# Moving five blocks of h and the forget sums to other turns of a hand-written order (decoder layer, f32, one core)

## The chip, the cores and the metric

The kernel runs on one core of a Trainium2 chip. The time is that of the device in microseconds (us) for one launch, median of several runs. In the profile, PE is TensorE's matmuls and PEld its weight loads, DVE is VectorE, ACT ScalarE, POOL GpSimd, and SP the engine that issues most DMAs; a q behind a name is the engine's queue of issues.

## The reference

One layer of a decoder over 256 tokens of width 2048: a projection into the inputs of three kinds of mixers, their outputs projected back, and an MLP.

```python
mod = (silu(c) @ w_mod[l] + b_mod[l])[:, None, :]
sh1, sc1, g1, sh2, sc2, g2 = jnp.split(mod, 6, axis=-1)
h = rms_norm(x, norm1_g[l]) * (1.0 + sc1) + sh1
(fq, fk, fv, ff, nq, kc, vc, ksl, vsl, kwn, vwn, ng, ca, cg) = split_in(h @ w_in[l])
log_f = jax.nn.log_sigmoid(ff + b_f[l])
o_fox = fox_attention(hd(fq), hd(fk), hd(fv), log_f)   # adds F[t] - F[s], F = cumsum(log_f)
o_nsa = nsa_attention(...)
o_conv = conformer_conv(ca, cg, ...)
x = x + g1 * (concat([o_fox, o_nsa, o_conv]) @ w_out[l])
h = rms_norm(x, norm2_g[l]) * (1.0 + sc2) + sh2
x = x + g2 * (jnp.square(jax.nn.relu(h @ w_mlp1[l])) @ w_mlp2[l])
```

## The kernel before

All products with weights are made in three parts, high by high, high by low and low by high, in a 32-bit format of TensorE (fp32r). So each piece of weights that arrives in `raw` is split: ScalarE copies it into `w_hi` (`weight_hi`, line 749), and VectorE takes the difference into `w_lo` (`weight_lo`, line 1497). The unit of this is a half: 1024 columns of 128 rows, two rows of tiles deep. There are four buffers each of `w_hi` and `w_lo`, so ScalarE may write `w_hi` of half n when TensorE has done half n-4. TensorE takes 24 matmuls of 256 columns for a half that gives results by feature (lines 1059 to 1061), 12 matmuls of 512 columns for one by token (lines 1083 to 1085), and short ones of 176 columns for the group TL.

The input projection has 88 halves. They go in units over quarters of the depth: halves 0 to 21 use blocks 0 and 1 of h (a block is two tiles of 128 features), halves 22 to 37 blocks 2 and 3, halves 38 to 45 blocks 4 and 5, halves 46 to 53 blocks 6 and 7, and from half 54 on units use several. TL has halves 20, 21, 28 and 29 in the stretch of interest.

The order of all engines is written out by hand. TensorE goes through slots, with half n in slot n. ScalarE, VectorE and SP go through turns; in turn n they treat half n of the weights, some three halves ahead of TensorE. Each engine does its instructions in order, and what it needs of another it waits for by semaphore. In a turn:

- ScalarE first copies the result of a unit that has ended, then makes a block of h if `H_AT` names one for this turn (`scale_shift`, lines 754 to 765), then writes `w_hi`, then makes the four products of a tap of the convolution (`conv_products`, line 789, turns 56 and on).
- VectorE adds the result of a unit that has ended, writes `w_lo`, adds a tap (line 1604), splits the block that ScalarE made a turn before (`split_h`, line 1552), and last takes products with modulation weights.

A block of h needs the modulation's shift and scale as columns. VectorE makes them: `modulation_column` (line 1504) multiplies 128 rows of `w_mod` with the row of silu(c) and sums (2.2 us), four of them make a block, and behind the fourth VectorE's `scale_shift` writes `scale_h` (line 1529) and counts up `col_ok`. By `MODS_AT` there is one such product in each odd turn and two in turns 9, 21, 27 and 33. The fourth product of blocks 2 to 7 falls into turns 9, 17, 23, 29, 35 and 43. ScalarE's part begins so:

```python
def scale_shift(b):
    act.wait_ge(col_ok, b + 1)
    act.wait_ge(xt_ok, b + 1)
    if b >= 2:
        act.wait_ge(h_ready, b - 1)
```

The forget gates' running sums are eight small matmuls (`forget_sums`, lines 1264 to 1274) in slot `F_SLOT`. In turn `F_SLOT + AHEAD` (AHEAD is 3) VectorE splits them into `f_split` (lines 1785 to 1797). The first scores of the FoX heads, in slot 72, wait for that (`f_sb`, line 1219), as `f_split` is an operand of theirs. VectorE then adds the mask and takes the maximum (line 1632, first in turn 75), ScalarE takes the exponential (line 812), and TensorE transposes (line 1244) in slot 73.

All weights are issued by SP on one queue in the order of the turns: in each odd turn two halves of weights (1 MB), behind a wait for a `w_lo` that frees `raw`, and for each product of modulation weights the next load into its buffer (1 MB, line 550), behind a wait for that product.

Of the kernel before, what the change touches and what calls it, by code (L numbers as in the profile page):

```python
# [126 lines left out]
TAIL_TURN = TAIL_SLOT + AHEAD  # L127

LF_TURN = FIRST_HALF[UNITS.index((FE, 3, 1, 2, False, True)) + 1] + 4
F_SLOT = 64  # L130
MIX_SLOTS = [FOX_AT + 6, FOX_AT + 10, FOX_AT + 14, NSA_SLOT + 14, NSA_SLOT + 17, TAIL_SLOT + 1]
GATE_SLOTS = [NSA_SLOT + t for t in (18, 19, 20, 21)]
MIX_TURNS = [n + AHEAD for n in MIX_SLOTS]
# [62 lines left out]
    return 32 + 2 * i  # L196


H_AT = {12: 2, 20: 3, 27: 4, 33: 5, 39: 6, 45: 7}


def view(ap, dims, shift=0):
# [4 lines left out]
def build(nc, x_d, c_d, wmod_d, bcol_d, bmod_d, n1_d, n2_d, fg_d, main_d, tail_d, bf_d, wck_d, wcv_d, pos_d,  # L207
# [6 lines left out]
    with ctx:  # L214
# [484 lines left out]
        def _(act):  # L699
# [54 lines left out]
# [6 lines that stand above are left out]
                for k in (2 * b, 2 * b + 1):  # L760
                    A(h_f[b % 2][:, (k % 2) * S:(k % 2 + 1) * S], xn_t[:, k, :], ACT.Identity,
                      bias=m_sum[:, 2 * k:2 * k + 1], scale=scale_h[:, k:k + 1]).then_inc(h_ok, 1)
                act.wait_ge(h_ok, 2 * b + 2)
                A(act_hi[:, 2 * b:2 * b + 2, :], h_f[b % 2][:, :].rearrange("p (k t) -> p k t", k=2), ACT.Copy)\
                    .then_inc(h_hi, 1)
# [87 lines left out]
            for turn, (half, step) in enumerate(TURNS):  # L853
# [9 lines left out]
                if turn == TAP_HALF - 1:  # L863
                    act.wait_ge(small_in, 16 * N_SMALL)
                    act.wait_ge(evac_add, added(CG))
                    A(conv_y[:, :, :], conv_y[:, :, :], ACT.Sigmoid).then_inc(conv_sig, 1)
                if turn in H_AT:
                    scale_shift(H_AT[turn])
                if half is not None:
# [179 lines left out]
        def _(pe):  # L1049
# [214 lines left out]
            def forget_sums():  # L1264

                pe.wait_ge(lf_ok, 1)
                pe.wait_ge(evac_add, added(FE))
                for base in (0, HD):
                    out = spare[base:base + NFOX, 0:3 * P]
                    mm(out[:, 0:P], log_f[:, 0, :], tri[:, :], start=True, stop=True)  # L1270
                    mm(out[:, P:2 * P], log_f[:, 0, :], tri[:, :], start=True, stop=True)
                    mm(out[:, 2 * P:3 * P], log_f[:, 0, :], ones[:, :], start=True, stop=False)
                    last = mm(out[:, 2 * P:3 * P], log_f[:, 1, :], tri[:, :], start=False, stop=True)
                last.then_inc(f_ps, 1)
# [43 lines left out]
            for slot, (half, step) in enumerate(SLOTS):  # L1318
# [17 lines left out]
                if slot == 3:  # L1336
                    pe.wait_ge(bias_row, 1)
                if slot == F_SLOT:
                    forget_sums()
# [142 lines left out]
        def _(dve):  # L1482
# [66 lines left out]
            def split_h(b):  # L1549
                dve.wait_ge(h_hi, b + 1)  # L1550
                src = h_f[b % 2][:, :].rearrange("p (k t) -> p k t", k=2)
                TTn(act_lo[:, 2 * b:2 * b + 2, :], src, act_hi[:, 2 * b:2 * b + 2, :].bitcast(f32),
                    ALU.subtract).then_inc(h_ready, 1)
# [34 lines left out]
            def add_tap(tap):  # L1588

                if tap < 0:  # L1590
                    dve.wait_ge(conv_sig, 1)
                    TTn(conv_in[:, :, CONV_W - 1:], conv_in[:, :, CONV_W - 1:], conv_y[:, :, :], ALU.mult)\
                        .then_inc(conv_sem, 1)
                elif tap in VECTOR_TAPS:
                    dve.wait_ge(conv_sem, tap)
                    for ct in range(CT):
                        last = STT(conv_y[:, ct, :], conv_in[:, ct, tap:tap + S], convw[:, ct, tap:tap + 1],
                                   conv_y[:, ct, :], ALU.mult, ALU.add)
                    last.then_inc(conv_sem, 1)
                elif tap > 0:  # L1600
                    n = SCALAR_TAPS.index(tap)
                    dve.wait_ge(conv_tap, n + 1)
                    dve.wait_ge(conv_sem, tap)
                    TTn(conv_y[:, :, :], conv_y[:, :, :], conv_p[n % 2][:, :, :], ALU.add).then_inc(conv_sem, 1)  # L1604
# [133 lines left out]
            for turn, (half, step) in enumerate(TURNS):  # L1738
# [21 lines left out]
                if 0 < turn - TAP_HALF - 1 < CONV_W:  # L1760
                    add_tap(turn - TAP_HALF - 1)
                if turn - 1 in H_AT:
                    split_h(H_AT[turn - 1])
                if turn == LF_TURN:
# [5 lines left out]
                if turn == LF_TURN + 2:  # L1770
# [13 lines left out]
                    STT(log_f[:, :, :], s, -2.0, lf[0][:, :, :], ALU.mult, ALU.add).then_inc(lf_ok, 1)  # L1784
                if turn == F_SLOT + AHEAD:

# [365 lines left out]
```

## Time and profile before

| | |
|---|---|
| median of 3 runs | 1215.96 us (1215.74 to 1217.17) |
| profiled execution, its own time | 1217.17 us |
| its span, first to last instruction | 1215.4 us |
| mean granted TensorE clock | 0.975 of 2.4 GHz |
| TensorE busy | 1163.8 us, 96% |
| VectorE busy | 896.3 us, 74% |
| ScalarE busy | 605.8 us, 50% |

The span is from the first instruction to the last; the execution's time holds 1.8 us around it. A granted clock of 0.50 means 1.2 GHz. Busy shares are means over stages of different kinds; the input projection is the first 280 us or so.

### The profile page before, as it was taken

How to read it: one execution, taken by the hardware profiler on the slowest of the kernel's cores; microseconds unless marked ns; L12 is line 12 of the kernel's file. 1: busy time of each engine (PE TensorE's matmuls, PEld its weight loads, DVE VectorE, ACT ScalarE, POOL GpSimd, SP SyncE). 2: the span in 40 equal slices, each digit the busy share in tenths (PEclk: the TensorE clock that was granted, in tenths of full speed). 3: DMA queues.
4: the chain of work that ended last, by engine and by line, in shares of the span. 5: the costliest groups of instructions: out<-in, count | busy, mean ns of one | idle time of the engine just before them, and what ended most of it. 6: DMA issues, size and time to landing. Idle time of an engine off the chain costs nothing.

```text
span 1215.4 us, 17307 instructions
## 1 busy us (share of the span) xinstructions
PE 1163.8 (96%) x6807; PEld 1009.9 (83%) x6807; DVE 896.3 (74%) x1011; ACT 605.8 (50%) x874; POOL 10.5 (1%) x29
## 2 busy tenths in 40 slices
PE   4999999999999996999999999999999999999997
PEld 4899989988877775999788888888888888888785
DVE  5998999998889978896865666545666545667674
ACT  6655448876754544544433444433444433444452
POOL 2000000000000000000000000000000000000000
PEclk6999999999989997999999999999999999999998
DMA  9999996538856875986667664555665456665441
GB/s 380 419 420 420 420 365 251 179 142 295 277 208 250 298 317 210 355 308 242 231 229 261 242 236 179 186 195 210 259 225 204 173 196 238 238 227 178 169 173 69
DMA packets 45752, 306.11 MB, mean 252 GB/s; under 512 B 6316, under 2 KB 7928, under 8 KB 9208
## 3 DMA queue, kind: packets, MB, share of 16 engines
q1 hardware_dynamic: 43728, 302.58, 66.0%
q10 hardware_dynamic: 1896, 2.64, 0.8%
q8 instruction: 43, 0.70, 0.2%
q14 instruction: 21, 0.17, 0.0%
q0 software_dynamic: 64, 0.02, 0.0%
HBM read 303.10 MB, written 2.12 MB: 251 GB/s over the span
## 4 chain that ended last, share of the span: by engine, by line
PE 77%; DVE 10%; ACT 5%; issue 5%; DMA 3%; SPq 0%; DVEq 0%; ACTq 0%
PE quad L1069 15%; PE quad L1083 12%; PE quad L1085 12%; PE quad L1084 12%; PE quad L1071 7%; PE quad L1059 5%; PE quad L1060 5%; PE quad L1061 5%; DMA mod_raw<-in_w_mod 3%; DVE w_lo L1497 2%; ACT w_hi L749 2%; DVE mod_raw L1504 2%; DVE conv_y L1604 1%; ACT score L812 1%; ACT conv_p L789 1%
## 5 line engine op out<-in xcount | busy, mean ns | idle before, releaser
L1497 DVE TENSOR_TENSOR w_lo<-raw,w_hi 128x1024 fp32r<-128x1024 f32 (+1 forms) x372 | 446.8, 1208 | 263.8 <-ACT w_hi L749 263.2
L749 ACT ACTIVATE w_hi<-raw 128x1024 fp32r<-128x1024 f32 (+1 forms) x372 | 387.4, 1045 | 424.0 <-PE quad L1085 218.9
L1069 PE MATMUL quad<-act,w_hi 128*128 128x512 f32 x768 | 268.1, 394 | 0.0
L1059 PE MATMUL quad<-act,w_hi 128*128 128x256 f32 x768 | 223.1, 291 | 8.7 <-DVE w_lo L1497 4.6
L1060 PE MATMUL quad<-act,w_hi 128*128 128x256 f32 x768 | 220.8, 287 | 0.0
L1061 PE MATMUL quad<-act,w_lo 128*128 128x256 f32 x768 | 220.7, 287 | 0.0
L1071 PE MATMUL quad<-act,w_lo 128*128 128x256 f32 x768 | 215.4, 280 | 0.0
L1083 PE MATMUL quad<-w_hi,u_hi 128*128 128x512 f32 x496 | 196.4, 396 | 0.5 <-DVE u_lo L1914 0.5
L1085 PE MATMUL quad<-w_hi,u_lo 128*128 128x512 f32 x496 | 195.9, 395 | 0.0
L1084 PE MATMUL quad<-w_lo,u_hi 128*128 128x512 f32 x496 | 195.9, 395 | 0.0
L1069 PEld LDWEIGHTS quad<-act,w_hi 128*128 128x128 f32 x768 | 144.2, 188 | 33.4
L1059 PEld LDWEIGHTS quad<-act,w_hi 128*128 128x128 f32 x768 | 150.1, 195 | 11.5 <-issue 8.8
L1060 PEld LDWEIGHTS quad<-act,w_hi 128*128 128x128 f32 x768 | 150.2, 196 | 0.2
L1061 PEld LDWEIGHTS quad<-act,w_lo 128*128 128x128 f32 x768 | 150.0, 195 | 0.0
L1071 PEld LDWEIGHTS quad<-act,w_lo 128*128 128x128 f32 x768 | 144.5, 188 | 0.1
L1083 PEld LDWEIGHTS quad<-w_hi,u_hi 128*128 128x128 f32 x496 | 93.0, 187 | 23.8 <-DVE u_lo L1914 0.9
L1084 PEld LDWEIGHTS quad<-w_lo,u_hi 128*128 128x128 f32 x496 | 93.0, 187 | 22.7 <-issue 0.2
L1085 PEld LDWEIGHTS quad<-w_hi,u_lo 128*128 128x128 f32 x496 | 93.0, 187 | 22.7
L1504 DVE CUSTOM_DVE_ANT_0 mod_raw<-mod_raw,acc 128x2048 f32<-128x2048 f32 x40 | 91.3, 2287 | 12.7 <-ACT acc L725 7.6
L1515 DVE SCALAR_TENSOR_TENSOR acc<-mod_raw,c_act,acc 128x2048 f32<-128x2048 f32 x32 | 75.1, 2346 | 0.0
L812 ACT ACTIVATE score<-score,neg_max 128x128 f32<-128x128 f32 x72 | 31.9, 444 | 52.5 <-DVE neg_max L1632 52.5
L789 ACT ACTIVATE conv_p<-conv_in,convw 128x256 f32<-128x256 f32 x108 | 45.8, 496 | 8.9 <-DVE conv_y L1604 8.9
(288 smaller groups left out, 1161.0 us busy)
## 6 DMA issues: line engine op xcount, KB each, us to landing
raw<-in_w_main SPq DMA_DIRECT2D x184, 1024.0 KB, 4.8
mod_raw<-in_w_mod SPq DMA_DIRECT2D x72, 1024.0 KB, 6.6
first_raw<-in_w_mod SPq DMA_DIRECT2D x14, 1024.0 KB, 14.1
late_raw<-in_w_mod SPq DMA_DIRECT2D x10, 1024.0 KB, 7.6
x_a<-in_x SPq DMA_DIRECT2D x2, 1024.0 KB, 6.9
x<-in_x SPq DMA_DIRECT2D x2, 1024.0 KB, 8.6
out<-raw SPq DMA_DIRECT2D x4, 512.0 KB, 3.1
bias_t<-bias_scratch ACTq DMA_DIRECT2D x1, 1536.0 KB, 15.2
```

Source lines behind the costliest of these rows:

```text
L749: A(dst[:, 0:2 * width], block_half(raw, j, width), ACT.Copy).then_inc(hi_done, 1)
L1059: mm(out, hi, act_hi[:, k, :], start=begin and m % 2 == 0, stop=False, skip_group_check=True)
L1060: mm(out, hi, act_lo[:, k, :], start=False, stop=False, skip_group_check=True)
L1061: last = mm(out, lo, act_hi[:, k, :], start=False, stop=end, skip_group_check=True)
L1069: mm(out, w_hi[j % 4][:, cols], act_both[:, k, :, :].rearrange("p h t -> p (h t)"), start=begin, stop=False, skip_group_check=True)
L1071: last = mm(out[:, 0:S], w_lo[j % 4][:, cols], act_hi[:, k, :], start=False, stop=end, skip_group_check=True)
L1083: mm(out, t_hi, hi, start=begin, stop=False)
L1084: mm(out, t_hi, lo, start=False, stop=False)
L1085: last = mm(out, t_lo, hi, start=False, stop=end)
L1497: TTn(lo[:, 0:2 * width], block_half(raw, j, width), hi[:, 0:2 * width].bitcast(f32), ALU.subtract)\
L1504: v.tensor_tensor_reduce(out=src[:, :], in0=src[:, :], in1=acc[0][:, :], scale=1.0, scalar=0.0, op0=ALU.mult, op1=ALU.add, accum_out=m_col ...
L1515: STT(out, src[:, :], c_act[:, bass.ds(k, 1)], out, ALU.mult, ALU.add).then_inc(mod_step, 1)
```

## The change

Two constants of the written order are changed. The keys of `H_AT` are the turns in which ScalarE makes a block, the values the blocks; VectorE's `split_h` comes one turn after.

```diff
-F_SLOT = 64
+F_SLOT = 70
 MIX_SLOTS = [FOX_AT + 6, FOX_AT + 10, FOX_AT + 14, NSA_SLOT + 14, NSA_SLOT + 17, TAIL_SLOT + 1]
 GATE_SLOTS = [NSA_SLOT + t for t in (18, 19, 20, 21)]
...
-H_AT = {12: 2, 20: 3, 27: 4, 33: 5, 39: 6, 45: 7}
+H_AT = {12: 2, 18: 3, 24: 4, 30: 5, 36: 6, 44: 7}
```

Which block is made in which turn, and when its columns are made and the block is needed:

| block | columns, VectorE's turn | made, before | made, after | first needed by half |
|---|---|---|---|---|
| 2 | 9 | 12 | 12 | 22 |
| 3 | 17 | 20 | 18 | 23 |
| 4 | 23 | 27 | 24 | 38 |
| 5 | 29 | 33 | 30 | 39 |
| 6 | 35 | 39 | 36 | 46 |
| 7 | 43 | 45 | 44 | 47 |

## Rows read from the trace of the kernel before

**Rows 1.** The page: the span, and TensorE's busy time.

```profile
span 1215.4 us, 17307 instructions
...
PE 1163.8 (96%) x6807; PEld 1009.9 (83%) x6807; DVE 896.3 (74%) x1011; ACT 605.8 (50%) x874; POOL 10.5 (1%) x29
```

**Rows 2.** Waits, 50 to 155 us: us in total, times, longest.

```profile
DVE mod_raw L1504 <- DMA mod_raw<-in_w_mod: 2.8, 4, 1.5
...
PE quad L1059 <- DVE w_lo L1497: 2.3, 1, 2.3
```

**Rows 3.** Timeline of ScalarE: start, us, operation, count, [idle before, releaser].

```profile
90.14 1.06 ACT L749 ACTIVATE w_hi<-raw 128x1024 fp32r<-128x1024 f32 x1 [0.25 <-PE quad L1085]
...
99.71 1.43 ACT L749 ACTIVATE w_hi<-raw 128x1024 fp32r<-128x1024 f32 x2
...
105.72 1.06 ACT L749 ACTIVATE w_hi<-raw 128x1024 fp32r<-128x1024 f32 x1 [1.49 <-PE quad L1061]
...
112.16 1.09 ACT L761 ACTIVATE h_f<-xn_t,m_sum,scale_h 128x256 f32<-128x256 f32 x2 [0.39 <-DVE scale_h L1529]
...
113.82 1.04 ACT L749 ACTIVATE w_hi<-raw 128x1024 fp32r<-128x1024 f32 x1
...
123.78 1.06 ACT L749 ACTIVATE w_hi<-raw 128x1024 fp32r<-128x1024 f32 x1 [1.78 <-PE quad L1061]
...
132.22 1.06 ACT L749 ACTIVATE w_hi<-raw 128x1024 fp32r<-128x1024 f32 x1
```

**Rows 4.** Timeline of VectorE, 83 to 131 us.

```profile
83.69 0.53 DVE L1497 TENSOR_TENSOR w_lo<-raw,w_hi 128x352 fp32r<-128x352 f32 x1 [1.19 <-ACT w_hi L749]
...
94.03 2.35 DVE L1497 TENSOR_TENSOR w_lo<-raw,w_hi 128x1024 fp32r<-128x1024 f32 x2
...
100.79 1.23 DVE L1497 TENSOR_TENSOR w_lo<-raw,w_hi 128x1024 fp32r<-128x1024 f32 x1 [1.05 <-ACT w_hi L749]
...
106.80 0.68 DVE L1552 TENSOR_TENSOR act<-h_f,act 128x512 fp32r<-128x512 f32 x1
...
109.43 2.29 DVE L1504 CUSTOM_DVE_ANT_0 mod_raw<-mod_raw,acc 128x2048 f32<-128x2048 f32 x1 [1.51 <-DMA mod_raw<-in_w_mod]
...
112.04 2.35 DVE L1497 TENSOR_TENSOR w_lo<-raw,w_hi 128x1024 fp32r<-128x1024 f32 x2
...
121.83 2.29 DVE L1504 CUSTOM_DVE_ANT_0 mod_raw<-mod_raw,acc 128x2048 f32<-128x2048 f32 x1 [0.65 <-DMA mod_raw<-in_w_mod]
...
129.53 2.36 DVE L1497 TENSOR_TENSOR w_lo<-raw,w_hi 128x1024 fp32r<-128x1024 f32 x2
```

**Rows 5.** Timeline of TensorE, and a window with its granted clock (PEclk).

```profile
113.41 0.36 PE L1059 MATMUL quad<-act,w_hi 128*128 128x256 f32 x1 [2.30 <-DVE w_lo L1497]
...
115.27 0.41 PE L1059 MATMUL quad<-act,w_hi 128*128 128x256 f32 x1
...
115.00:116.00 1.00, 1.00 (x7) 1.00 (x6) 1.00 (x1) 0.00 (x0) 0.00 (x0) 0.50 1.08 451
```

**Rows 6.** SP's issue, and a window (last two: DMA share, GB/s).

```profile
98.63 0.33 SPq L550 DMA_DIRECT2D mod_raw<-in_w_mod  x1
...
100.00:104.00 4.00, 4.00 (x36) 4.00 (x35) 3.21 (x2) 2.32 (x4) 0.00 (x0) 1.00 1.02 420
```

**Rows 7.** Timelines of TensorE and VectorE around the first scores.

```profile
216.62 0.38 PE L1059 MATMUL quad<-act,w_hi 128*128 128x256 f32 x1
...
222.03 0.17 DVE L1790 CAST neg_id_r<-neg_id 128x12 fp32r<-128x12 f32 x1
...
225.00 1.23 DVE L1497 TENSOR_TENSOR w_lo<-raw,w_hi 128x1024 fp32r<-128x1024 f32 x1
...
239.53 0.44 PE L1231 MATMUL quad<-f_split,neg_id_r 44*128 44x384 f32 x2
...
243.54 0.28 DVE L1632 CUSTOM_DVE_ANT_0 score<-quad,causal 128x128 f32<-128x128 f32 x1
...
245.25 0.55 PE L1244 MATMUL quad<-ident,score 128*128 128x128 f32 x3 [1.59 <-ACT score L812]
```

## The prediction

> **What bounds the kernel now.** I read the page first. TensorE is busy for 1163.8 of 1215.4 us, so what the change does to the end is what it does to TensorE's waits and clock [rows 1]. The change touches two stretches of the input projection, so I listed the waits of 50 to 155 us. TensorE waits there for a single thing: 2.3 us, for a `w_lo` of VectorE; and VectorE waits 2.8 us in all for modulation weights to land [rows 2]. I then put the timelines of ScalarE and VectorE side by side and gave each `w_hi` and `w_lo` its number by counting turns. TensorE runs half n in slot n; ScalarE writes `w_hi` of half n once half n-4 is done (so a `w_hi` that waited for TensorE tells when that half ended), and VectorE then writes `w_lo` of half n. VectorE is the full engine: two `w_lo` (1.14 us each from start to start), a product of modulation weights (2.2 us) and now and then a `split_h` (0.60) stand against two halves of TensorE (5.6 to 5.7 us), and in four turns of the stretch there are two products. So TensorE sets the pace with VectorE about a microsecond ahead of it, and any idle time of VectorE over that goes to TensorE.
>
> The one stall shows the pattern. VectorE waits 1.51 us for weights to land, starts the product at 109.43, and starts `w_lo` of half 30 at 112.04 [rows 4]; TensorE, idle since about 110.94, starts half 30 at 113.41, 1.37 us after that `w_lo` began, and then runs at a granted clock of 0.50, 1.2 of 2.4 GHz, for 3.4 us [rows 5]. Seventeen matmuls came 0.213 apart where 0.118 is usual, so the lower clock costs another 1.6 us behind the 2.3.
>
> **H_AT, removed and added.** No operation is added or taken away. Blocks 3 to 7 of h are made at turns 18, 24, 30, 36, 44 where they were at 20, 27, 33, 39, 45, and their `split_h` moves with them. TensorE needs them much later (halves 23, 38, 39, 46, 47), so being earlier is worth nothing by itself. What matters is what `scale_shift` on ScalarE waits for: the columns `scale_h` of its block, which VectorE writes at the end of turns 17, 23, 29, 35 and 43. Four of the five moves put the block into the very next turn (18, 24, 30, 36), and so does 44. In before, ScalarE runs ahead: it wrote `w_hi` of half 24 at 90.14, of half 30 at 105.72 and of half 36 at 123.78 [rows 3], while VectorE started the `w_lo` behind the columns of these blocks at 94.03, 112.04 and 129.53 [rows 4]. In the changed kernel these `w_hi` stand on ScalarE behind a wait for those columns. Queued behind the waiting instruction are `w_hi` of that half and the next ones, and VectorE's next instruction is the `w_lo` of just that half: the two engines, which ran side by side, run one after the other.
>
> The price of one such place comes from block 5 in turn 33. From the start of the product (109.43) to `h_f` on ScalarE (112.16) are 2.73 us, from there to the next `w_hi` (113.82) 1.66 [rows 3, 4], and a `w_lo` starts 1.08 behind its `w_hi` (99.71 and 100.79): 5.47 us. Today it is 2.61 (109.43 to 112.04). So VectorE idles 2.86 us more at each of turns 18, 24, 30, 36, and at 44 too, where the cover is greater.
>
> Against that, VectorE loses idle time it has now: 1.19 us at half 21 (it waits for ScalarE, which waits for TensorE), 1.05 at half 27 (ScalarE was at block 4 in that turn), 1.51 and 0.65 for weights to land [rows 4]: 4.4 us, which are swallowed by its being late. 0.73 us comes on at half 31, as in that turn a copy of a result stands between `w_hi` 30 and 31 on ScalarE. I carried it through turn by turn, as shift against before of the start of each operation:
> - `w_lo` 18: +2.86. `w_lo` 20: +3.48 (its `split_h` is now ahead of it). `w_lo` 22: +1.61 (1.19 swallowed, `split_h` gone from behind 21, small gaps). It starts at 90.77; TensorE gets it at 92.14 and is ready at 91.24: a stall of 0.9.
> - `w_lo` 24: +4.49, start 98.52, TensorE gets it at 99.89 and is ready at 97.82: a stall of 2.1.
> - `w_lo` 27: +3.96. Product before block 5: at 111.21, the landing wait of 1.51 gone: +1.78. `w_lo` 30: +4.64, start 116.68. TensorE gets it at 118.05 where it got it at 113.41: it is 4.6 us behind before, whatever its clock did in between, as this chain is on VectorE and ScalarE alone.
> - `w_lo` 32: +5.89; `w_lo` 34: +5.17 (landing wait of 0.65 and small gaps swallowed); `w_lo` 35: +4.57; `w_lo` 36: +7.43, start 136.96.
> TensorE gets half 36 at 138.33. Today it starts it at 131.98 (ScalarE saw half 35 end at 132.22 [rows 3], less 0.24, the lag seen at half 30), 1.08 after it could. So TensorE is 7.43 - 1.08 = 6.35 us late there. It would be ready at 136.6, with the lower clock after half 30 in it: a stall of about 1.7. The stall of 1.59 us at 245.25 is followed by the lower clock as well [rows 7], so I add 1.6: +8.0 us from half 37 on. At turn 44 the columns come late once more; `w_lo` 44 reaches TensorE at 160.2, and it needs it at 160.9 at the earliest: no stall. From turn 47 VectorE again waits for ScalarE and TensorE, so all three are 8.0 us late, and nothing later is tied to a fixed time that could give it back. Of the clock I can bound only this: 0 if the last stall is too short, 1.6 if not, 3.3 if it takes two such stretches.
>
> One thing is tied to fixed times: weights land by their place in the queue. The product's weights were issued at 98.63 and landed at 109.43, 10.8 us later [rows 6], while the DMA share is above 1.00 throughout (this issue alone moves 1 MB, 2.5 us at 420 GB/s): the rest is backlog. In the changed kernel that issue comes about 5 us later, at 103.7, behind a queue that is still full until 106.9, so I leave the landing at 109.43, before the 111.21 at which it is wanted. The Trainium skill (DMA: Bandwidth & Descriptors, section "Two DMAs through the same engine are not ordered") says that within one queue of one engine descriptors start in order though they are pipelined. By this the landing is set by the bytes ahead, and the sum stays as it is; were the 10.8 us a latency of its own, the landing would be 114.5 and the sum 3.3 us more.
>
> The skill has a rule that speaks for a smaller sum: TensorE: Matmul & The Clock Gate, section "Why this matters for your kernels", ties drops of throughput in mid-kernel to idle gaps longer than any in my list. By it none of my stalls costs clock, and the sum would be 6.35. The row at 113.41 shows otherwise after 2.30 us, and the measurement decides.
>
> **F_SLOT.** The eight forget sums (1.42 us of TensorE, up to the start of half 64 at 216.62) and VectorE's six passes for `f_split` (2.97 us, 222.03 to 225.00) move six turns on, to slot 70 and turn 73 [rows 7]. What has to wait for them is the first score in slot 72, which started at 239.53. Told on before's times: without the passes `w_lo` 68 to 73 move up, but VectorE then soon waits for ScalarE, whose turn of tap products takes 2.55 us where VectorE's takes 2.27, so that `w_lo` 73 starts at 235.9 instead of 238.71, the tap behind it ends at 238.17 and `f_split` at 241.14. The scores start at 241.37 where TensorE is free at 239.35: a new wait of 2.0 us. The bias of these scores starts on VectorE at 243.42, before at 243.54. TensorE has a wait of 1.59 us in front of the transposes at 245.25 and a lower clock behind it; both are now spent one slot earlier: half 72 ends at 245.24 + 1.7 = 246.9, and the transposes stand where they stood in effect (245.25 + 1.7). I take 0. Bounds: -1.15, all of VectorE's idle time from 222.03 to 243.54, and +2.0, if the new wait is added whole.
>
> **Sum.** 6.35 + 1.6 + 0 = +8.0 us. The profiled execution took 1217.17 us around its span of 1215.4, 1.2 above the median of 1215.96; so I expect 1225.2 for that one and 1224.0 for the median.
>
> **Rivals.**
> - *The serial turns, but the clock holds* after the last stall: 6.35, 1222.3. For it: that stall is the shortest of the three large ones. Against it: 245.25.
> - *Dearer*: landings move with their issue (+3.3), the slot 72 wait is added whole (+2.0), or a second slow stretch (+1.7): 1226 to 1229.
> - *Half of it hidden*: VectorE's margin ahead of TensorE takes up more than the 1.08 us that I counted, or one of the turns isn't serial: 1219 to 1221.
> - *No change, the blocks' wait hidden*: that wants the columns before the `w_hi`; the row at 112.16 with its 0.39 us of waiting, three turns later than it would be asked, is against it. 1216.
> - *Faster*: with block 4 out of turn 27 VectorE saves its wait of 1.05 at half 27, and with its `split_h` (0.60 at 106.80) out of turn 28 it is 1.65 us earlier at `w_lo` 30; the stall of 2.30 falls to 0.65 and the 1.6 of clock go with it: 1215.96 - 3.25 = 1212.7. This decides only if the columns of block 5 are there before about 105.7, where `w_hi` 30 stands, 6.4 us earlier than the trace has them.
>
> **How the numbers follow.** Forecast 0.55, clock holds 0.14, dearer 0.11, half hidden 0.09, no change 0.05, faster 0.06. A change under 0.2% (2.4 us) can't be told from none here. Slower is 0.89, same 0.05, faster 0.06. The range from 1219.5 to 1228.5 leaves out the last two, the lower edge of the half-hidden case and the upper one of the dear case.
>
> **What would show it.** Right: ScalarE's `h_f` waits for `scale_h` at blocks 3 to 7, each time followed by a `w_lo` that waits about 2.9 us for `w_hi`; waits of TensorE for `w_lo` at halves 24, 30 and 36 of 2.1, 2.6 and 1.7 us and a granted clock of 0.50 behind each; half 36 at 138.3; from turn 50 everything later by one constant; a wait of 2.0 us before the first score. The prediction is wrong if landings of weights end VectorE's waits, if half 36 starts before 136, or if the 8 us are there at 160 and gone at 460.

## The result

| | before | after |
|---|---|---|
| median, us | 1215.85 (6 runs, 1214.73 to 1217.17) | 1221.16 (6 runs, 1220.16 to 1223.61) |
| ratio, 95% interval | | 1.0051, 1.0040 to 1.0062 |
| profiled execution, its own time | 1217.17 | 1221.82 |
| its span | 1215.4 | 1220.1 |
| mean granted clock | 0.975 | 0.979 |

The changed kernel is 0.5% slower, 5.3 us by the medians, where 8.0 were forecast. The ratio is taken over all 15 of its timed runs, whose mean is 1222.0 us; by it the difference is 6.2 us, with an interval of 4.9 to 7.5. For the same reason a ratio and a difference of medians below can differ by some tenths of a us. The page of after, against [rows 1]:

```profile
span 1220.1 us, 17307 instructions
...
PE 1159.6 (95%) x6807; PEld 1005.9 (82%) x6807; DVE 895.7 (73%) x1011; ACT 604.0 (50%) x874; POOL 10.5 (1%) x29
```

TensorE's busy time is even 4.2 us lower, since it spent less time at the low clock and had a faster pace late in the kernel (see *Spans* below). The longer span is idle time. The waits from 50 to 155 us (us in total, times, longest), against [rows 2]:

```profile
ACT h_f L761 <- DVE scale_h L1529: 27.4, 5, 7.5
...
DVE w_lo L1497 <- ACT w_hi L749: 11.7, 5, 2.8
PE quad L1059 <- DVE w_lo L1497: 7.0, 3, 3.9
...
PE quad L1083 <- DVE w_lo L1497: 1.5, 1, 1.5
...
DVE mod_raw L1504 <- DMA mod_raw<-in_w_mod: 0.6, 2, 0.4
```

TensorE waits 8.5 us for `w_lo` where it waited 2.3. VectorE's waits for weights have shrunk from 2.8 to 0.6 us, swallowed by its lateness. ScalarE now stands before a block of h for up to 7.5 us. Its timeline, at blocks 4 and 5, against [rows 3]:

```profile
95.59 1.09 ACT L761 ACTIVATE h_f<-xn_t,m_sum,scale_h 128x256 f32<-128x256 f32 x2 [6.48 <-DVE scale_h L1529]
...
97.25 2.94 ACT L749 ACTIVATE w_hi<-raw 128x1024 fp32r<-128x1024 f32 x3
...
113.70 1.09 ACT L761 ACTIVATE h_f<-xn_t,m_sum,scale_h 128x256 f32<-128x256 f32 x2 [6.64 <-DVE scale_h L1529]
```

And VectorE's, against [rows 4]: the `w_lo` of halves 18, 24, 30 and 36, each behind the same wait.

```profile
80.21 2.36 DVE L1497 TENSOR_TENSOR w_lo<-raw,w_hi 128x1024 fp32r<-128x1024 f32 x2 [2.78 <-ACT w_hi L749]
...
98.33 2.36 DVE L1497 TENSOR_TENSOR w_lo<-raw,w_hi 128x1024 fp32r<-128x1024 f32 x2 [2.77 <-ACT w_hi L749]
...
110.98 2.28 DVE L1504 CUSTOM_DVE_ANT_0 mod_raw<-mod_raw,acc 128x2048 f32<-128x2048 f32 x1
...
116.43 1.23 DVE L1497 TENSOR_TENSOR w_lo<-raw,w_hi 128x1024 fp32r<-128x1024 f32 x1 [2.77 <-ACT w_hi L749]
...
136.67 2.36 DVE L1497 TENSOR_TENSOR w_lo<-raw,w_hi 128x1024 fp32r<-128x1024 f32 x2 [2.77 <-ACT w_hi L749]
...
249.67 0.29 DVE L1632 CUSTOM_DVE_ANT_0 score<-quad,causal 128x128 f32<-128x128 f32 x1
```

The row at 113.70 is the pattern in one line: ScalarE had been ready for 6.64 us, VectorE wrote the columns, waited 2.77 us for the `w_hi` behind them, and only then had work again. TensorE, against [rows 5, 7], with three windows of it (the third number from the end is the granted clock):

```profile
91.96 0.36 PE L1059 MATMUL quad<-act,w_hi 128*128 128x256 f32 x1 [1.36 <-DVE w_lo L1497]
...
99.70 0.36 PE L1059 MATMUL quad<-act,w_hi 128*128 128x256 f32 x1 [1.81 <-DVE w_lo L1497]
...
117.80 0.36 PE L1059 MATMUL quad<-act,w_hi 128*128 128x256 f32 x1 [3.87 <-DVE w_lo L1497]
...
138.04 0.48 PE L1083 MATMUL quad<-w_hi,act 128*128 128x512 f32 x1 [1.54 <-DVE w_lo L1497]
...
211.13 0.36 PE L1059 MATMUL quad<-act,w_hi 128*128 128x256 f32 x1 [2.27 <-DVE w_lo L1497]
...
247.30 0.44 PE L1231 MATMUL quad<-f_split,neg_id_r 44*128 44x384 f32 x2 [3.08 <-DVE f_split L1795]
```

```profile
100.00:101.00 1.00, 1.00 (x11) 1.00 (x10) 1.00 (x2) 1.00 (x2) 0.00 (x0) 1.00 0.96 401
...
120.00:122.00 2.00, 2.00 (x12) 2.00 (x11) 2.00 (x2) 0.50 (x1) 0.00 (x0) 0.50 0.89 340
...
139.00:140.00 1.00, 1.00 (x6) 0.77 (x6) 1.00 (x3) 0.48 (x1) 0.00 (x0) 1.00 0.32 131
```

There are four waits at halves 22, 24, 30 and 36, as worked out, but the clock fell behind one of them alone, that of 3.87 us (it fell once more behind the 3.08 us before the first scores). Half 36 starts at 138.04. In the projection TensorE is then 6.1 us late; the wait at half 61 stands at 211.13 where it stood at 205.00, and the first mask and maximum at 249.67 where it was at 243.54, both 6.13 us later.

### The profile page after: what moved, and what is told of

It is laid out like the page before. It is cut to its first block, busy times and chain, and to the rows that moved or that the text cites. A ratio compares the mean times of both kernels' runs of the same rounds, so it can differ in the third digit from the quotient of the medians.

```text
span 1220.1 us, 17307 instructions
## 1 busy us (share of the span) xinstructions
PE 1159.6 (95%) x6807; PEld 1005.9 (82%) x6807; DVE 895.7 (73%) x1011; ACT 604.0 (50%) x874; POOL 10.5 (1%) x29
## 4 chain that ended last, share of the span: by engine, by line
PE 70%; DVE 15%; ACT 7%; issue 5%; DMA 3%; SPq 0%; DVEq 0%; ACTq 0%
PE quad L1069 14%; PE quad L1083 11%; PE quad L1084 11%; PE quad L1085 11%; PE quad L1071 7%; DVE w_lo L1497 4%; PE quad L1059 3%; PE quad L1060 3%; PE quad L1061 3%; DVE mod_raw L1504 3%; ACT w_hi L749 2%; DMA mod_raw<-in_w_mod 2%; DVE first_raw L1504 2%; DVE conv_y L1604 1%; ACT conv_p L789 1%
```

## The experiments

Each was timed against the kernel before on the same chip. The medians of before were 1215.88 us beside the two parts apart, the repeat and block 6 alone; 1215.78 beside block 3 alone, all blocks one turn later and the first move of modulation products; and 1215.59 beside the other four. Theory A is that of the prediction: ScalarE and VectorE run one after the other in the turns in which a block waits for its columns, and VectorE's loss less what its later idle time swallows goes to TensorE. Its main rival B puts the cost to the new wait before the first scores.

### The two parts apart

```diff
-H_AT = {12: 2, 20: 3, 27: 4, 33: 5, 39: 6, 45: 7}
+H_AT = {12: 2, 18: 3, 24: 4, 30: 5, 36: 6, 44: 7}
```

> The five blocks are moved and the forget sums stay in slot 64. Theory A (the serial turns of VectorE and ScalarE carry all of the change): VectorE's wait for w_hi at halves 18, 24, 30 and 36 is 2.8 us each, TensorE starts half 36 at about 138.0 as in the changed kernel, and the time is 4.5 to 6.5 us over before. Rival B (the cost is the new wait of 3.08 us in front of the first scores): the time is within 2.4 us of before. Clock: the waits of TensorE at halves 22, 24 and 36 (1.4, 1.8, 1.5 us) will be followed by the lower clock in some executions and not in others, so this run need not match the changed kernel's profile there.

Measured 1222.27 us, ratio 1.0057 (1.0045 to 1.0070), 6.4 us over before. TensorE starts half 36 at 138.12.

```diff
-F_SLOT = 64
+F_SLOT = 70
```

> The forget sums are moved to slot 70 and the blocks stay where they were. Theory A: a new wait of TensorE of 2.0 to 3.1 us for f_split before the first scores, the wait of 1.59 us before the first transposes gone, the first mask and maximum on VectorE (before at 243.54) within 0.3 us of that, and the time within 1.2 us of before. Rival B: the new wait is added whole, 2 to 3 us over before.

Measured 1216.20 us, ratio 1.0001 (0.9992 to 1.0010). Its timeline of TensorE has the new wait before the first scores:

```profile
242.63 0.69 PE L1231 MATMUL quad<-f_split,neg_id_r 44*128 44x384 f32 x2 [3.09 <-DVE f_split L1795]
```

A wait of 3.09 us that costs nothing: the mask and maximum stands at 245.00, 38.56 us behind the end of the wait at half 61 (206.44). In before these are 38.54 (243.54 less 205.00), in after 38.54 (249.67 less 211.13). I had expected that row within 0.3 us of the 243.54 of before, and missed it: the whole execution was 1.44 us later from half 61 on. The wait of 1.59 us at the transposes is gone, as expected. Rival B falls: the blocks alone give all of the change's cost, and the forget sums none that shows within an interval of -1.0 to 1.2 us.

### The changed kernel once more

> The changed kernel itself again, for another sample of the clock. Theory C (which of the short waits is followed by the lower clock is chance, not set by the length of the wait): waits of the same length at halves 22, 24, 30 and 36 within 0.2 us where no fall comes before them, and another set of falls behind them than in the first profile (there: behind 3.87 us yes, behind 1.36, 1.81 and 1.54 no). Rival D (a wait is followed by a fall from some length on): the same set. Time 1220 to 1224.

Measured 1222.83 us, ratio 1.0060 (1.0048 to 1.0072). TensorE's waits in the new profile, and a window behind the first:

```profile
92.21 0.36 PE L1059 MATMUL quad<-act,w_hi 128*128 128x256 f32 x1 [1.34 <-DVE w_lo L1497]
...
99.95 0.36 PE L1059 MATMUL quad<-act,w_hi 128*128 128x256 f32 x1 [0.29 <-DVE w_lo L1497]
...
118.07 0.55 PE L1059 MATMUL quad<-act,w_hi 128*128 128x256 f32 x1 [3.86 <-DVE w_lo L1497]
...
138.31 0.47 PE L1083 MATMUL quad<-w_hi,act 128*128 128x512 f32 x1 [0.72 <-DVE w_lo L1497]
...
247.59 0.44 PE L1231 MATMUL quad<-f_split,neg_id_r 44*128 44x384 f32 x2 [1.54 <-DVE f_split L1795]
...
93.00:94.00 1.00, 1.00 (x6) 1.00 (x6) 1.00 (x2) 0.00 (x0) 0.00 (x0) 0.50 1.01 421
```

The same 1.3 us of waiting at half 22 is followed by the clock of 0.50 here and was not in the first profile. TensorE lost time to it, and found `w_lo` 24 nearly ready: 0.29 us of waiting and not 1.81. Halves 30 and 36 start 25.86 and 46.10 us after half 22, against 25.84 and 46.08 in the first profile. So ScalarE and VectorE set these starts, and a low clock between two waits costs nothing there; only one behind the last wait would. That holds even for the wait at half 30, in which the clock fell before it ended and stayed low for 6.8 us, twice as long as in the first profile. Behind half 36 the clock held in all three profiles of these blocks (after, its repeat, the blocks alone; the waits there were 1.54, 0.72 and 1.53 us). Rival D falls for the short waits. All of TensorE's waits over 1 us between 85 and 255 us, in the profiles of before, after, its repeat and the two parts apart, and then in all thirteen profiles of this case (a fall is counted that came in the wait or up to 1.6 us behind it):

| wait, us | clock fell, these five | clock fell, all thirteen |
|---|---|---|
| 1.25 to 1.69 (halves 22, 30, 32, 34 and 36, scores) | in 2 of 7 | in 5 of 15 |
| 1.81 to 1.97 (halves 24 and 30) | in 1 of 2 | in 3 of 4 |
| 2.26 to 2.34 (halves 30, 36 and 61) | in 4 of 7 | in 10 of 17 |
| 2.53 to 2.55 (scores) | in 1 of 1 | in 2 of 4 |
| 2.91 to 3.87 (half 30, scores) | in 5 of 5 | in 7 of 7 |

### One block alone

```diff
-H_AT = {12: 2, 20: 3, 27: 4, 33: 5, 39: 6, 45: 7}
+H_AT = {12: 2, 20: 3, 27: 4, 33: 5, 36: 6, 45: 7}
```

> Only block 6 is moved, from turn 39 to 36. Theory A: one serial turn, 2.8 us of new waiting of VectorE for w_hi at half 36, of which TensorE's distance of 1.08 us takes a part: TensorE waits 1.7 to 1.8 us at half 36 for w_lo, and the time is 1.3 to 2.0 us over before, 3.4 with the lower clock behind the wait. Rival (the cost needs all moves together, one is absorbed): 0.

Measured 1218.16 us, ratio 1.0014 (1.0005 to 1.0023), over before by 2.3 us by the medians and 1.7 by the ratio. VectorE's wait is there:

```profile
132.56 2.36 DVE L1497 TENSOR_TENSOR w_lo<-raw,w_hi 128x1024 fp32r<-128x1024 f32 x2 [2.77 <-ACT w_hi L749]
```

TensorE waits 0.89 us and not 1.7 for it in this profile, since its own wait at half 30 was 3.05 us, the clock fell in it and stayed low for 6.8 us, and that had made TensorE later. The interval of 0.6 to 2.8 us holds the 1.8 of the sum and leaves out the rival's 0.

```diff
-H_AT = {12: 2, 20: 3, 27: 4, 33: 5, 39: 6, 45: 7}
+H_AT = {12: 2, 18: 3, 27: 4, 33: 5, 39: 6, 45: 7}
```

> Only block 3 is moved, from turn 20 to 18. Theory A (a serial turn costs only what VectorE's later idle time does not swallow): TensorE gets a new wait of about 0.9 us at half 22, VectorE's waits of 1.05 us at half 27 and of 1.51 us for the weights that land at 109.43 shrink by as much, the wait of TensorE at half 30 shrinks from 2.30 to about 1.4 us, half 30 starts at 113.4 as before, and the time is that of before within 1 us. Rival (each serial turn costs its own 1.8 us): 1.5 to 2 us over before.

Measured 1214.62 us, ratio 0.9989 (0.9980 to 0.9997): no cost, 1.2 us less if anything. The timeline of VectorE:

```profile
80.67 2.36 DVE L1497 TENSOR_TENSOR w_lo<-raw,w_hi 128x1024 fp32r<-128x1024 f32 x2 [2.78 <-ACT w_hi L749]
...
102.03 1.23 DVE L1497 TENSOR_TENSOR w_lo<-raw,w_hi 128x1024 fp32r<-128x1024 f32 x1 [0.40 <-ACT w_hi L749]
...
109.63 2.29 DVE L1504 CUSTOM_DVE_ANT_0 mod_raw<-mod_raw,acc 128x2048 f32<-128x2048 f32 x1 [0.47 <-DMA mod_raw<-in_w_mod]
```

And that of TensorE:

```profile
92.42 0.36 PE L1059 MATMUL quad<-act,w_hi 128*128 128x256 f32 x1 [0.72 <-DVE w_lo L1497]
...
113.60 0.36 PE L1059 MATMUL quad<-act,w_hi 128*128 128x256 f32 x1 [1.25 <-DVE w_lo L1497]
```

The same 2.78 us of VectorE's time is lost, and paid back from the waits at half 21 (gone, 1.19 in before), at half 27 (0.40 for 1.05) and for weights (0.47 for 1.51). The product starts at the landing, 109.63 (in before 109.43), and half 30 starts at 113.60. TensorE's one wait of 2.30 is split into 0.72 and 1.25 and no low clock follows in this profile. From the start of half 30 to the end of the wait at half 61 are 90.74 us here (204.34 less 113.60) and 91.59 in before, so the missing fall is worth 0.85 us. The profile is ahead by more than that at its end, 3.3 us; half of it, 1.7 us, comes from a faster pace of TensorE behind 664 us that doesn't go with the blocks (see *Spans* below). Whether the 1.2 us of the medians are real isn't shown.

### The place of the wait

```diff
-H_AT = {12: 2, 20: 3, 27: 4, 33: 5, 39: 6, 45: 7}
+H_AT = {12: 2, 19: 3, 25: 4, 31: 5, 37: 6, 45: 7}
```

> Blocks 3, 4, 5, 6, 7 in turns 19, 25, 31, 37, 45, one turn after the changed kernel's, with the forget sums in slot 64. Theory A: when ScalarE waits for the columns, the w_hi of the turn in which they are made is already there, so VectorE does one w_lo (1.14 us) in the meantime and waits 1.7 us and not 2.8 in each of four places. 4 x 1.7 less the 4.4 that are swallowed, less the distance of 1.08: 1 to 3 us over before, so well under the time of the kernel with all moves. Rival (what costs is that the blocks are early at all): 4.5 to 6.5 us over before.

Measured 1216.41 us, ratio 1.0004 (0.9995 to 1.0013), 0.6 us over before where 1 to 3 were expected. VectorE waits 1.63 to 1.65 us for `w_hi` in the four places; at block 4:

```profile
97.54 1.23 DVE L1497 TENSOR_TENSOR w_lo<-raw,w_hi 128x1024 fp32r<-128x1024 f32 x1 [1.65 <-ACT w_hi L749]
```

One turn makes 5.8 us of difference to the blocks alone in the changed kernel's turns.

Now with the changed kernel's turns and ScalarE's order within a turn reversed:

```diff
-H_AT = {12: 2, 20: 3, 27: 4, 33: 5, 39: 6, 45: 7}
+H_AT = {12: 2, 18: 3, 24: 4, 30: 5, 36: 6, 44: 7}
...
-                if turn in H_AT:
-                    scale_shift(H_AT[turn])
                 if half is not None:
                     weight_hi_in(half)
+                if turn in H_AT:
+                    scale_shift(H_AT[turn])
```

> The blocks in the changed kernel's turns 18, 24, 30, 36, 44, the forget sums in slot 64, and one edit: in each turn ScalarE writes w_hi first and makes the block behind it. Theory A (the cost is that w_hi of just the half that VectorE wants next stands behind the wait for the columns): each serial turn leaves VectorE waiting 1.6 us and not 2.8, as with all blocks one turn later, and the time is within 2 us of before, 4 to 6 us under the kernel with the same turns and the old order. Rival (it is the turns in which the blocks stand): 1221 to 1223 as with the old order.

Measured 1217.70 us, ratio 1.0021 (1.0012 to 1.0031), 2.1 us over before: just outside of the 2 us expected, and 4.3 us less over its before than the blocks alone in the old order. VectorE's waits are 1.64, 1.65, 2.55 and 1.64 us, the second of them:

```profile
97.25 1.23 DVE L1497 TENSOR_TENSOR w_lo<-raw,w_hi 128x1024 fp32r<-128x1024 f32 x1 [1.65 <-ACT w_hi L749]
```

It is not the turns, but what stands behind the wait. The 2.55 at half 31, where a copy of a result comes in between, I hadn't counted.

```diff
-H_AT = {12: 2, 20: 3, 27: 4, 33: 5, 39: 6, 45: 7}
+H_AT = {12: 2, 20: 3, 26: 4, 32: 5, 38: 6, 45: 7}
```

> Blocks 4, 5 and 6 one turn before where the kernel before has them (26, 32, 38), nothing else. Theory A: the columns of all three are written or nearly so when ScalarE comes there, so no wait of VectorE for w_hi over 1.7 us appears; the wait of 1.05 us at half 27 goes; the weights still land at 109.4 to 109.8 and set half 30; the time is that of before within 1.2 us.

Measured 1216.22 us, ratio 1.0006 (0.9998 to 1.0015): no difference, as expected. VectorE's wait at half 27 is gone and comes back in front of the weights (2.83 us for 1.51). They land at 109.52, and half 30 starts where it did:

```profile
113.50 0.55 PE L1059 MATMUL quad<-act,w_hi 128*128 128x256 f32 x1 [2.91 <-DVE w_lo L1497]
```

This answers the prediction's rival *Faster* as well: with block 4 out of turn 27 half 30 is no earlier, as the product before it has to wait for the landing.

### Whether another order is faster

```diff
+MODS_AT = {turn + (turn == 29): n for turn, n in MODS_AT.items()}
```

> Before with one edit: the product with modulation weights of turn 29 (the one that VectorE waits for until 109.43) is done at the end of turn 30, behind w_lo of half 30. Theory A (VectorE does its work in order, and w_lo 30 stands behind a load that lands late): w_lo 30 starts at about 107.9 and not at 112.04, the wait of TensorE at half 30 (2.30 us) goes, w_lo 31 is just in time, and with the lower clock behind it 2.3 to 4 us are saved: 1212 to 1213.7. Rival (the wait only moves on to half 31 or 32, since VectorE's work is the bound there): within 1 us of before.

Measured 1214.74 us, ratio 0.9988 (0.9979 to 0.9997), where 1212 to 1213.7 were expected. The wait at half 30 is gone, and two others have come, at halves 32 and 34 (the next expectation miscounts the second as 35):

```profile
118.27 0.36 PE L1060 MATMUL quad<-act,w_hi 128*128 128x256 f32 x1 [1.50 <-DVE w_lo L1498]
...
125.73 0.47 PE L1084 MATMUL quad<-w_hi,act 128*128 128x512 f32 x1 [1.54 <-DVE w_lo L1498]
```

They are 3.04 us in all for 2.30, so the 1.0 us that the median gains isn't less waiting. In this profile the clock fell behind neither of them nor at half 61; in before it fell at halves 30 and 61. That may be where the gain comes from, but one profile doesn't show it.

```diff
+MODS_AT = {turn: n for turn, n in MODS_AT.items() if turn not in (29, 31, 33)} | {30: 1, 32: 1, 33: 1, 34: 1}
```

> Before with the products of turns 29, 31 and 33 (one, one, two) in turns 30, 32, 33 and 34 (one each), so that w_lo of the half that TensorE wants is not behind a load that lands late. With the product of turn 29 alone moved, the wait of 2.30 us at half 30 went and waits of 1.50 and 1.54 us at halves 32 and 35 came. Theory A (the order of work decides): those shrink to 1 us or less in sum, 1212.5 to 1214. Rival (VectorE with the landing times is the bound of this stretch, the order only moves the waits): 1214 to 1215.5.

Measured 1214.94 us, ratio 0.9997 (0.9988 to 1.0006). The waits have moved on once more, to halves 35 (125.69, 0.47 us) and 36 (131.04, 2.31 us). With blocks 3 and 4 at turns 19 and 26 as well:

```diff
-H_AT = {12: 2, 20: 3, 27: 4, 33: 5, 39: 6, 45: 7}
+H_AT = {12: 2, 19: 3, 26: 4, 33: 5, 39: 6, 45: 7}
```

> As the run before, and blocks 3 and 4 at turns 19 and 26. If the order decides, no slower than the run before, and ScalarE's block is out of turn 27; if landings decide, the same within 0.8 us. A price of the serial turn at 19 (1.6 us of VectorE) should be swallowed by waits for weights behind it.

Measured 1216.64 us, ratio 1.0003 (0.9993 to 1.0014). This is 1.7 us over the run before and so fits neither expectation, though the intervals of the two ratios overlap. In its profile the clock fell behind all three waits of TensorE over 1 us (131.11, 205.76 and 246.01), in that of the run before behind one, which may be the difference. The rival holds as far as the first two of these kernels show it: moving the products moves the waits about (2.30; 1.50 and 1.54; 0.47 and 2.31) and takes none away, so the stretch is bound by VectorE's work with the landing times. No version beat the kernel before by more than the 0.2% that can be told here; the two lowest ratios are 0.9988 and 0.9989, with intervals up to 0.9997.

## Why the prediction was right, and its one wrong term

- *The serial turns.* Right in kind, place and size. VectorE idles 2.77 to 2.78 us at halves 18, 24, 30 and 36 where 2.86 more were worked out; `w_lo` 24, 30 and 36 start at 98.33, 116.43 and 136.67 against 98.52, 116.68 and 136.96; half 36 starts at 138.04 against 138.33. At half 44 VectorE waits 2.78 us as well (159.24), and no wait of TensorE follows, as forecast. Undoing the order in the turn and moving the blocks by one turn took away 4 to 6 us, and the blocks alone gave all of it.
- *What swallows it.* Right: the waits at halves 21 and 27 and for the weights are gone in after; block 3 alone costs nothing, block 6 alone, behind which no such idle time stands, does.
- *The landing.* Right: with block 3 alone the load was issued at 100.52, 1.89 us later than in before, and the product started at its landing, 109.63 for 109.43. In after the load was issued at 103.53 and the product of block 5's columns is at 110.98 (111.21 worked out) with no wait, 7.5 us later; a latency of 10.8 us from the issue, which would have added 3.3 us, falls by that.
- *The waits of TensorE.* At half 22 1.36 for 0.9, at half 24 1.81 for 2.1, at half 30 3.87 for 2.6, at half 36 1.54 for 1.7. The one at 22 came out longer since TensorE was 0.6 us earlier in this execution (ready at 90.60 for the 91.22 of before), the one at 30 since the low clock that I had put behind half 24 did not come. A clock of 0.50 behind each of 24, 30 and 36 was named as a sign of being right; it came behind 30 alone.
- *The clock behind half 36*, "so I add 1.6: +8.0 us". This is the term that was mis-sized: it measured 0 in all three profiles. The single row I had, a wait of 1.59 us before the transposes with a low clock behind it, was one throw. At its own place it was a fair guide, as the clock fell at waits of 1.58 to 1.69 us there in 4 of 6 profiles; at halves 22, 32, 34 and 36 it fell at 1 of 7 waits of 1.34 to 1.54 us. Without the term the sum is 6.35 us, and the three measurements of these blocks are 5.3 (6.2 by the ratio), 6.9 and 6.4 us over their before. So what came true is the first rival, that the clock holds behind the last stall (6.35, 1222.3), which had a chance of 0.14, and not the forecast with its 0.55; the range was wide enough for both.
- *Spans.* After the projection the lateness was not a constant, as the prediction had it. Up to the wait before the MLP it rises, to 7.5 us (475.91 to 483.37 in the timelines), and then it falls to the 4.7 us of the spans, with the same waits behind that point in both profiles. The first 1.1 us are back at 663.82 (670.15 in after); the low clock around that wait lasts 2.5 us less behind it in after, which at half the pace gives an estimate of 1.2. The other 1.7 us come back up to 774.78 (779.43 in after), and not by the granted clock, which is 1.00 in both:

```profile
690.00:750.00 60.00, 60.00 (x342) 52.10 (x340) 42.80 (x34) 28.16 (x28) 0.00 (x0) 1.00 0.59 213
```

```profile
690.00:750.00 60.00, 60.00 (x348) 52.73 (x347) 42.53 (x34) 28.52 (x28) 0.00 (x0) 1.00 0.59 215
```

The first row is of before, the second of after: 342 matmuls start in the same 60 us where 348 do. Of the thirteen profiles five have the slower pace (before, the blocks alone, all blocks one turn later, the first move of modulation products, and the kernel with blocks 3 and 4 at 19 and 26) and eight the faster. Kernels with the same blocks are on both sides, and so are kernels with the forget sums in slot 64, so neither of the two edits sets it alone; what does stays open. The blocks alone and before share the slower one, and the difference of their medians is 6.4 us.
- *F_SLOT.* Right at 0, and the wait that moves forward by a slot was named; it is 3.08 us and not 2.0. The scores start where they were worked out (247.30 less 6.13 is 241.17, for 241.37), but TensorE was there sooner: my 239.35 was read from a profile with a low clock behind half 61, and in after none came there. In the repeat one did, and the wait is 1.54 us. Neither does harm, because the bias on VectorE is what the next step waits for: it stands 38.54 us behind the end of the wait at half 61 in before and in after, and 38.55 in the repeat.

## What to carry to other kernels

In an order written out by hand, look at what is queued behind a waiting instruction, not at when its result is wanted: each block made 3 to 14 halves before it was needed cost VectorE 2.8 us, because the next piece for the very engine that it waited for stood behind it; with that piece ahead of the wait it cost 1.6. An engine's lost time can be added up turn by turn from a trace, with its later idle time taken off; here its starts came out within 0.3 us over 60 us. A fall of the clock behind a short wait is a chance and not a term: count it once, at the last wait of a chain, and with the share that several profiles give.

## What the runs showed that was not expected

Waits of TensorE of the same length, 1.34 and 1.36 us at half 22 of the same kernel, were followed by a granted clock of 0.50 in one execution and by 1.00 in another; so were waits of 2.27 and 2.28 us at half 61. In the thirteen profiles it came at each of the seven waits of 2.91 us and more, and at 20 of the 40 between 1.25 and 2.55. A low clock between two waits that other engines set changed no start time: halves 30 and 36 kept their distance from half 22 within 0.02 us. And the same matmuls at the same granted clock of 1.00 have two paces between 690 and 750 us, 342 and 348 in 60 us, worth 1.7 us of the whole; a difference of that size between two single profiles need not come from the edit.
